# VectorE's routing step moved from behind the product with the gate to ahead of it, in the pick loop of a two-block forward pass

## What is computed

```python
def peer_ffn(h, w_pq, sub_keys, u_tab, v_tab):
    def chunk(xc):                                  # 128 tokens
        q = (xc @ w_pq).reshape(P_CHUNK, P_HEADS, 2, P_DK // 2)
        s = jnp.einsum('thpd,hpkd->thpk', q, sub_keys)
        s_top, i_top = lax.top_k(s, P_TOPK)         # 16 of 128, for each half key
        cand = s_top[..., 0, :, None] + s_top[..., 1, None, :]
        best, ci = lax.top_k(cand.reshape(P_CHUNK, P_HEADS, P_TOPK * P_TOPK), P_TOPK)
        e1 = jnp.take_along_axis(i_top[..., 0, :], ci // P_TOPK, axis=-1)
        e2 = jnp.take_along_axis(i_top[..., 1, :], ci % P_TOPK, axis=-1)
        expert = e1 * N_KEYS + e2
        gate = jax.nn.softmax(best, axis=-1)
        act = jax.nn.gelu(jnp.einsum('thkd,td->thk', u_tab[expert], xc))
        return jnp.einsum('thk,thkd->td', gate * act, v_tab[expert])
```

## Time and profile before

| | us |
|---|---|
| median of 3 runs | 2971.34 (2969.48 to 2979.59) |
| the profiled execution | 2971.38 |
| its span | 2970.1 |
| busy: PE, DVE, ACT, POOL | 2624.4, 1572.8, 651.5, 553.9 |
| pick loop, first dot | starts at 1617.62 |
| chain that ended last | PE 63%, DMA 26%, DVE 7%, ACT 2% |
| gathers | 536.90 MB |

### The profile page before, as it was taken

How to read it: one execution, slowest core, us unless ns; L and a number is a source line. 1 busy time by engine, 2 the same in 40 slices (tenths; PEclk the granted TensorE clock), 3 DMA queues, 4 the chain that set the end, 5 groups by cost and what they waited for, 6 DMA issues and landing times.

```text
span 2970.1 us, 23372 instructions
## 1 busy us (share of the span) xinstructions
PE 2624.4 (88%) x8074; PEld 1382.7 (47%) x8074; DVE 1572.8 (53%) x3510; ACT 651.5 (22%) x1573; POOL 553.9 (19%) x523
## 2 busy tenths in 40 slices
PE   8998899999999999999989988989877777777776
PEld 4684446666444444466657533535432323232222
DVE  1106335443106992266523686748675776658554
ACT  2114220001002002266511112222121221222111
POOL 0000000000000000000001434434444434444332
PEclk9997899999999999999989999999999999999999
DMA  3220023343222211000135999999999999999997
GB/s 139 100 85 1 22 85 142 142 162 121 106 73 93 85 62 68 14 1 28 51 120 227 392 360 413 406 420 420 420 419 420 420 420 420 420 420 420 420 420 293
DMA packets 87300, 686.95 MB, mean 231 GB/s; under 512 B 9976, under 2 KB 10616, under 8 KB 12816
## 3 DMA queue, kind: packets, MB, share of 16 engines
q0 software_dynamic: 73728, 536.90, 44.0%
q1 hardware_dynamic: 11408, 143.53, 12.7%
q10 hardware_dynamic: 2048, 5.03, 0.5%
HBM read 683.32 MB, written 2.10 MB: 231 GB/s over the span
## 4 chain that ended last, share of the span: by engine, by line
PE 63%; DMA 26%; DVE 7%; ACT 2%; issue 1%; POOL 0%; ACTq 0%; DVEq 0%
PE psum L346 34%; DMA weights<-in_experts,expert 13%; PE psum L909 11%; DMA slot<-in_experts,expert 8%; DMA xn<-in_experts,expert 5%; PE psum L842 3%; PE psum L751 3%; PE psum L703 2%; PE psum L809 2%; PE psum L773 2%; PE psum L824 1%; PE psum L759 1%; DVE weights L1848 1%; DVE slot L1848 1%; ACT spare_row L1305 1%
## 5 line engine op out<-in xcount | busy, mean ns | idle before, releaser
L909 PE MATMUL psum<-weights,spare_row 128*128 128x512 f32 x848 | 402.3, 619 | 120.7 <-ACT spare_row L1305 118.6
L909 PE MATMUL psum<-slot,spare_row 128*128 128x512 f32 x856 | 405.1, 617 | 96.8 <-ACT spare_row L1305 96.8
L346 PE MATMUL psum<-xnT,weights 128*128 128x257 f32 (+2 forms) x1568 | 423.9, 432 | 2.8 <-DVE xnT L1354 2.8
L346 PEld LDWEIGHTS psum<-xnT,weights 128*128 128x128 f32 x1568 | 298.8, 191 | 118.5 <-issue 82.2
L1904 POOL DMA_INDIRECT weights<-in_experts,expert x212 | 223.0, 1052 | 687.5 <-DVE expert L1814 351.6
L1848 DVE CUSTOM_DVE_ANT_0 slot<-slot,hT 128x1024 f32<-128x1024 f32 x214 | 260.5, 1223 | 155.1 <-DMA slot<-in_experts,expert 154.2
L1848 DVE CUSTOM_DVE_ANT_0 weights<-weights,hT 128x1024 f32<-128x1024 f32 x212 | 258.1, 1222 | 146.1 <-DMA weights<-in_experts,expert 145.4
L909 PEld LDWEIGHTS psum<-weights,spare_row 128*128 128x128 f32 x848 | 158.6, 195 | 354.3 <-ACT spare_row L1305 179.9
L909 PEld LDWEIGHTS psum<-slot,spare_row 128*128 128x128 f32 x856 | 161.4, 195 | 320.3 <-issue 166.1
L1904 POOL DMA_INDIRECT slot<-in_experts,expert x214 | 236.6, 1105 | 324.9 <-PE psum L909 312.9
L1300 ACT ACTIVATE coef<-hidden 128x2 f32<-128x2 f32 (+1 forms) x257 | 52.2, 203 | 984.0 <-DVE hidden L1848 984.0
(11 more groups left out here) (324 smaller groups left out, 2736.5 us busy)
## 6 DMA issues: line engine op xcount, KB each, us to landing
weights<-in_w_mod SPq DMA_DIRECT2D x12, 2048.0 KB, 8.7
weights<-in_w_up SPq DMA_DIRECT2D x11, 2048.0 KB, 7.7
weights<-in_w_in SPq DMA_DIRECT2D x8, 2048.0 KB, 8.7
weights<-in_w_pq SPq DMA_DIRECT2D x8, 2048.0 KB, 11.5
weights<-in_w_out SPq DMA_DIRECT2D x6, 2048.0 KB, 10.2
weights<-in_w_in_t SPq DMA_DIRECT2D x4, 2048.0 KB, 10.7
weights<-in_w_down SPq DMA_DIRECT2D x4, 2048.0 KB, 8.0
weights<-in_w_o_mla SPq DMA_DIRECT2D x4, 2048.0 KB, 8.6
```

What stands on the lines that cost most here:

```text
L346: last = pe.matmul(out, lhsT, rhs, start=start and n == 0, stop=stop and n == len(pairs) - 1)
L909: last = pe.matmul(acc.pair[:, half, :], k.diags[pick % 8], k.slots[slot][:, D + half * 512:D + (half + 1) * 512], start=h0 == 0 and j == ...
```

## The change

In `vector_program`, `peer()`: the steps of `beside` are drawn between the signal `hidden` of a group and the product with the gate, where they were drawn behind the product. The generator is given as many empty steps in front as a group draws, so that each step is made one group later, and keeps its place among the steps of its own row. `late` keeps its place behind the product. The other engines' programs are the same.

```diff
--- before.py
+++ after.py
@@ -1836,7 +1836,7 @@
         late = k.lagging(dense(1))
         pick = group = 0
         for b, (i, h0, nh) in enumerate(k.order):
-            beside = k.beside(b, finish_tile, route)
+            beside = chained(range(k.steps(b)), k.beside(b, finish_tile, route))
             hid, cf, g = k.hidden[b % 2], k.coef[b % 2], flat(k.gate[b % 2][:, 0:nh, :])
             for j0, size in k.groups(b):
                 group += 1
@@ -1848,12 +1848,12 @@
                     ins = dve.tensor_tensor_reduce(slot[:, 0:D], slot[:, 0:D], k.h2[:, i, :], 1.0, 0.0, ALU.mult, ALU.add, hid[:, j:j + 1])
                     pick += 1
                 ins.then_inc(s.hidden)
+                for _ in range(k.steps(b)):
+                    next(beside, None)
                 if j0 == 0:
                     dve.wait_ge(s.gated, b + 1)
                 dve.wait_ge(s.gelu, group)
                 dve.tensor_tensor(cf[:, cut], cf[:, cut], g[:, cut], ALU.mult).then_inc(s.coef)
-                for _ in range(k.steps(b)):
-                    next(beside, None)
                 next(late, None)
             for _ in beside:
                 pass
```

## The result

| | before | after |
|---|---|---|
| median of the runs of this comparison, us | 2973.59 (2967.01 to 2979.59, 17 runs) | 2978.95 (2972.86 to 2986.88, 17 runs) |
| ratio after/before | | 1.0021, interval 1.0012 to 1.003 |
| span of the profiled execution, us | 2970.1 | 2977.6 |

By the ratio the changed kernel is 6.2 us slower (0.21%; 3.6 to 8.9 us by the interval); the two medians lie 5.4 us apart. Both are inside the 0.3% that counts as no change here. Forecast were 2974.0 us and a loss of 2.7 us, and a range of 2967 to 2983 us. The time lies in the range. The sign is right, and the size is less than half of what was measured. The forecast was laid on a median of three runs, 2971.34 us; with 17 runs the kernel before has 2973.59 us, so 2.3 of the 5.0 us by which the time is off come from that base.

The account below looks back on a forecast made before the run. Gathers were taken to bound the loop from 1930 us on, TensorE or VectorE in windows before; 2971.4 + 2.4 (batch 0) - 1.0 (batch 1) + 1.4 (batch 2) = 2974.2 us, taken as 2974, range 2967 to 2983 us.

Parts of the forecast that it names:

- The frame: Pick loop: from 1930 us gathers set the pace at 419 or 420 GB/s; only earlier can VectorE edits move the end.
- Batch 0: +2.4 us: Six slots: steps behind late dots delay TensorE, 1.1 us at group 6, 1.3 by group 8, another 1.1 at group 11.
- The second half of the term: Batch 0, group 11: the route's last steps follow a late dot and cost another 1.1 us.
- Batch 1: -1.0 us: VectorE-bound batch: +1.4 us at group 3, then -2.4 us over nine products; bounds -2.4 and +1.4 us.
- The delay: Batch 1, group 3: the step of eight MAX, 1.65 us, stands behind a dot that waited: +1.4 us.
- The return: Batch 1, groups 4 to 12: nine products each give back the gelu wait of 0.27 us, -2.4 us.
- dearer table load: ScalarE's exponential: at the skill page's 2.66 us per table change, batch 1 would lose up to 3 us more; not summed.
- Batch 2: +1.4 us: Eight slots: the product of group 6 moves 1.9 us and part stays; bounds 0 (queue covers it) and +1.9 us.
- two returns of 0.27 us leave +1.35 us there: Batch 2, two groups after group 6: the queue runs short and +1.35 us of the product's 1.9 us shift remains.
- Tile change: 0: Tile 0 to 1: TensorE idles 6.5 us, slots return 6.0 and 7.5 us late, cover absorbs it; upper bound +2 us.
- the cover of 7.0 us: Eight-slot ring: median gather of 12.9 us less the shortest, 5.9 us, is lateness a slot release may have free.
- Rival 3: First tile change: late drain and half clock cost 7.5 us, total 2981.7; sign, below 415 GB/s behind 2000 us; chance 0.12.

Follow-up runs that it names:

- e13: The changed kernel, unchanged, profiled a third time; 2980.0 us, ratio 1.0027 to the kernel before.
- single-part kernels: Kernels moving only finish_tile's steps, only the route's, only batch 0's or only batch 1's, against before; ratios 1.0001, 1.0015, 1.0009, 1.0002.
- e6: Only batch 0 draws its steps ahead of the product and a group later, all else as before; 2975.99 us, ratio 1.0009.
- e10: The changed kernel, unchanged, profiled a second time; 2982.1 us, ratio 1.003 to the kernel before.
- e14: The changed kernel, unchanged, profiled a fourth time; 2978.73 us, ratio 1.0017 to the kernel before.
- e7: Only batch 1 draws its steps ahead of the product and a group later, all else as before; 2973.83 us, ratio 1.0002.
- e1: The kernel before, unchanged, profiled a second time; 2972.1 us, ratio 1.0001.
- e11: The kernel before, unchanged, profiled a third time; 2972.79 us, ratio 1.0001.
- e5: Against before, only finish_tile's steps (the drain among them) moved ahead of the product, two groups late; 2981.67 us, ratio 1.0021.
- e2: Against before, only finish_tile's steps (the drain among them) moved ahead of the product, one group late; 2973.93 us, ratio 1.0001.
- e12: The kernel before, unchanged, profiled a fourth time; 2974.72 us, ratio 1.0006.

## Why the prediction came out as it did

**The frame was right.** The gathers set the pace from 1930 us on: products 96 to 257 take 810.1 us in before and in after (809.6 in e13), and in each of the single-part kernels. No edit of VectorE's order touches this, and of 25.4 us of idle time taken away the median saw nothing. That is the reading of the earlier trace rows.

**Batch 0: +2.4 us, measured +1.8** (four profiles each; +2.4 in e6 alone, +2.6 by all fourteen). The mechanism, steps behind a late dot that hold up a TensorE without slack, is as forecast. Its place is not. Ahead of group 6 TensorE idled 0.16 and 0.23 us in e10 and e13 and not at all in after, e14 and e6, where 1.1 us were forecast: in after the second dot of that group stood 26.4 us behind the first product instead of 27.8 us, so the landing was 1.4 us earlier and paid for the step. The idling stood ahead of groups 7 to 10, 0.9 to 2.0 us in all. The second half of the term, another 1.1 us at group 11, is not seen as a longer wait there (3.37 to 4.21 us in after, 3.91 to 4.30 us in before); where TensorE lost time at that group, in after and e14, its matmuls took 6.15 and 6.31 us instead of 5.17 to 5.40 us. That the sum of two such halves came out near 2.4 us is in part luck.

**Batch 1: -1.0 us, measured -0.5,** with a scatter of 3 us between copies of before. The delay was mis-sized in e7 (+2.1 us by product 20 instead of +1.4), for want of the second late dot; in the four of after it is +1.6 us against the mean of before. The return was right in kind, 0.27 to 0.36 us against 0.27, but it came without fail at four of the nine products only; at the others it is there in some executions and outweighed by other waits in the rest. The three microseconds which a dearer table load would have cost batch 1 are in no profile: the four of after average 89.51 us. The page ScalarE: Activation LUTs of the Trainium skill (What ACT_TABLE_LOAD costs) charges 2.66 us with the drain; the stage times speak against paying it on the path here.

**Batch 2: +1.4 us, measured -0.5.** The queue covered it, which was the lower bound. The shift did come, and of the size that was forecast: product 38, that of group 6, stood 36.8 to 38.0 us behind product 32 in the four of after and 35.0 to 35.8 us in the four of before, +2.0 us against a forecast of 1.9. (One group earlier the landings scatter more: product 37 has 32.4, 31.0, 32.3 and 27.2 us in after, 26.8, 26.4, 27.1 and 29.5 us in before.) By product 58 nothing is left: 141.1 to 142.0 against 141.6 to 142.6 us. So 20 groups with eight slots brought the shift back. The step that failed is "two returns of 0.27 us leave +1.35 us there": it took a late product in front of a queue as lost, although the same prediction reckons 7.0 us of cover for eight slots.

**Tile change: 0, measured +1.8.** This is the step that failed by its reasoning. The wait was right, 6.54 us against 6.5. The matmuls behind it took 5.35 to 6.53 us in the four of after, not 6.66, so TensorE was done with the second slot 6.1 to 7.3 us late, not 7.5, and the first gather went out 6.3 us late, against 6.0 (5 us late by e1 and e11, where it goes out 9.9 and 10.1 us behind product 64). What was wrong is the cover of 7.0 us. It came from the median time of a gather with eight slots less the shortest of another stretch, with six (12.9 - 5.9 us). With a median, half the gathers have less; and by the prediction's own numbers, 7.5 us for the second slot, it was half a microsecond short, and 0 was put down all the same. If everything beyond the cover is lost one for one, the cover is 6.3 - 1.8 = 4.5 us by the mean of before, and 5.4 us by e5 (first gather 19.70 us behind product 64, so 11.0 us late, for a cost of 5.6 us). Both are estimates from these rows; by each the cover is 1.6 to 2.5 us less than the 7.0 us of the prediction. Rival 3 was right in kind (a slice of 413 GB/s behind 2000 us, below its mark of 415) and had a quarter of its price: 1.8 us instead of 7.5, since only a part of the lateness is lost. Together, two misses of opposite sign (batch 2 by -1.9 us, tile change by +1.8 us) left the sum of the loop at +2.5 us, against a forecast of +2.8. That the sum fits so well is luck.

**What the prediction did not have.** The timed runs say +6.2 us, the loops of the four profiles +2.5, the stages of all fourteen +3.6. The rest of the profiled difference lies ahead of the first product (+2.9 us), in code that is the same in both kernels. In single profiles it starts between 230 and 420 us. The windows of 256 to 333 us, of before, of after, and of e13, the same program as after:

```profile
256.00:333.00 77.00, 61.60 (x346) 36.13 (x345) 51.72 (x233) 41.17 (x132) 0.00 (x0) 0.74 0.00 1
```
```profile
256.00:333.00 77.00, 65.15 (x317) 37.50 (x316) 44.58 (x202) 36.22 (x115) 0.00 (x0) 0.63 0.00 1
```
```profile
256.00:333.00 77.00, 60.79 (x344) 35.59 (x344) 51.71 (x233) 41.14 (x132) 0.00 (x0) 0.77 0.00 1
```

The same code gets a granted clock of 0.63, 0.74 or 0.77, and with 0.63 it does 317 matmuls in the window instead of 344 to 346. Does this go with the change? e13 says not necessarily: 0.77, and a first product at 1619.98 us, as early as any of before. Nor does a late start make a slow median: e2 started the loop at 1628.83 us and e7 at 1624.43 us, and their medians are those of before. A profile is one execution of its set and need not be a typical one: that of e13, 2972.23 us, is the fastest of its seven, and that of e2, 2981.59 us, the slowest of its eleven. The timed runs of e13 are as slow as the other three sets of after (ratio 1.0027). So some 2.6 us of the 6.2 us are not accounted for by the stages that the change touches. With 3.6 us as the lower end of the interval and more than 1 us of uncertainty on the loops, they may be nothing but scatter. Whether they are that, or lie ahead of the loop, or in batches 0 and 1 of executions that weren't profiled, stays open.

## What to carry to other kernels

A step that is moved between two dependent operations fills a wait of the engine that makes it. This is worth something only where that engine is the bound: here 0.27 to 0.36 us a group, at four groups of batch 1. Wherever the engine waits for data, the step had cost nothing, and now stands on the path of all that hangs on the second operation.

Look at everything that is drawn from the same generator as the step that is meant. Here the drain of a sum came along, one group late, and held TensorE for 6.5 us. Where the cover of a ring of buffers is reckoned from a median, expect less of it: here it was some 2 us less than 7.0. Price what lies beyond it one for one as an upper bound; between one and two groups late it was 0.76 us for each.

## What the hardware showed that wasn't expected

- The same code ran at a granted clock of 0.63 to 0.77 of TensorE between 256 and 333 us, and the loop's first product came anywhere between 1619.1 and 1628.8 us in fourteen profiles of programs that are alike up to there. A profile of one execution doesn't rank two kernels that differ by less than that.
- The price of a restart of TensorE at the lower clock doesn't follow the length of the pause. Eight matmuls that take 3.70 us took 5.40 us behind 2.05 us of waiting in e1 and e11, and 3.70 us behind the same wait in before and e12; 3.70 us behind 3.56 us in e13; 5.76 us behind 6.54 us in after and 6.58 us in e2; and 5.26 us behind 11.53 us in e5.
- A queue of eight gathers gave back a shift of 2 us within 20 groups, in a stretch where the GB/s line stands at 406 to 420 already.
